# Five batches in place of eleven for the levels of a gated recurrence, with folded keys and queries copied into tiles of their own

## The reference, cut to what matters

```
f   = lb + (1 - lb) * sigmoid(z);   kin = 1 - f;   q = silu(q)
attn[i, j] = sum_k q[i, k] * kin[j, k] * prod_{j < t <= i} f[t, k]      (j <= i)
o[i]       = sum_j attn[i, j] * v[j]
o          = rms_norm(o) * gnorm * silu(g)
```

## Time and profile before

| what | value |
|---|---|
| median of 3 runs (lowest, highest) | 717.39 us (716.24, 717.43) |
| the profiled execution's own time | 716.37 us |
| its span, first to last instruction | 714.4 us |
| TensorE busy | 704.4 us, 99% of the span |
| VectorE, ScalarE, GpSimd busy | 439.6, 330.5, 139.3 us |
| granted TensorE clock, mean | 0.998 of full |

### The profile page before, as it was taken

How to read it: one execution, slowest core, us unless ns; L and a number is a source line. 1 busy time by engine, 2 the same in 40 slices (tenths; PEclk the granted TensorE clock), 3 DMA queues, 4 the chain that set the end, 5 groups by cost and what they waited for, 6 DMA issues and landing times.

```text
span 714.4 us, 10098 instructions
## 1 busy us (share of the span) xinstructions
PE 704.4 (99%) x3709; PEld 581.6 (81%) x3709; DVE 439.6 (62%) x706; ACT 330.5 (46%) x547; POOL 139.3 (20%) x106
## 2 busy tenths in 40 slices
PE   9999999999999999999999999999999999999995
PEld 6878878878888888888888888888888888888885
DVE  4774577697777655676766766767763333234546
ACT  5792534676676734534334333433332222226834
POOL 1015421076665512011011011011010000000000
PEclk9999999999999999999999999999999999999999
DMA  9433232332322114343333233333316232323202
GB/s 276 129 93 108 60 89 62 116 96 85 88 90 60 60 60 118 88 118 89 89 106 99 88 92 113 89 88 103 95 59 191 83 102 90 104 90 117 89 0 118
DMA packets 113454, 69.44 MB, mean 97 GB/s; under 512 B 2946, under 2 KB 108370, under 8 KB 113418
## 3 DMA queue, kind: packets, MB, share of 16 engines
q1 hardware_dynamic: 111406, 65.42, 30.8%
q10 hardware_dynamic: 2012, 3.52, 1.5%
HBM read 66.81 MB, written 2.13 MB: 96 GB/s over the span
## 4 chain that ended last, share of the span: by engine, by line
PE 95%; DVE 3%; issue 1%; ACT 1%; POOL 0%; DVEq 0%; ACTq 0%
PE bank L640 24%; PE bank L641 24%; PE bank L642 24%; PE bank L646 4%; PE bank L648 4%; PE bank L647 4%; PE bank L838 2%; PE bank L822 2%; PE bank L810 1%; PE bank L697 1%; PE bank L812 1%; PE bank L880 1%; PE bank L1062 0%; DVE b_kq L541 0%; PE bank L755 0%
## 5 line engine op out<-in xcount | busy, mean ns | idle before, releaser
L1122 ACT ACTIVATE w_hi<-raw 128x1024 fp32r<-128x1024 f32 (+1 forms) x104 | 107.9, 1039 | 221.0 <-PE bank L642 202.4
L640 PE MATMUL bank<-h_hi,w_hi 128*128 128x512 f32 x518 | 203.6, 393 | 0.0
L642 PE MATMUL bank<-h_hi,w_lo 128*128 128x512 f32 x518 | 202.0, 390 | 0.0
L641 PE MATMUL bank<-h_lo,w_hi 128*128 128x512 f32 x518 | 201.8, 390 | 0.0
L1572 DVE TENSOR_TENSOR w_lo<-raw,w_hi 128x1024 fp32r<-128x1024 f32 (+1 forms) x104 | 128.9, 1240 | 103.3 <-ACT w_hi L1122 103.2
L642 PEld LDWEIGHTS bank<-h_hi,w_lo 128*128 128x128 f32 x518 | 97.2, 188 | 20.6
L640 PEld LDWEIGHTS bank<-h_hi,w_hi 128*128 128x128 f32 x518 | 97.3, 188 | 20.2 <-issue 0.9
L641 PEld LDWEIGHTS bank<-h_lo,w_hi 128*128 128x128 f32 x518 | 97.3, 188 | 18.7
L2147 POOL TENSOR_SCALAR probs<-probs,row_inv 128x512 f32<-128x512 f32 (+3 forms) x48 | 67.1, 1403 | 65.4 <-DVE row_inv L1824 65.4
L2157 POOL TENSOR_TENSOR conv_v<-conv_g,conv_v 128x512 f32<-128x512 f32 x22 | 28.3, 1288 | 212.9 <-DVE conv_v L1701 212.9
L640 PE MATMUL bank<-act_hi,w_hi 128*128 128x512 f32 x176 | 68.6, 389 | 0.0
(11 more groups left out here) (279 smaller groups left out, 1032.5 us busy)
## 6 DMA issues: line engine op xcount, KB each, us to landing
raw<-in_w_up SPq DMA_DIRECT2D x44, 512.0 KB, 3.7
raw<-in_w_in SPq DMA_DIRECT2D x18, 512.0 KB, 3.8
raw<-in_w_down SPq DMA_DIRECT2D x16, 512.0 KB, 3.5
raw<-in_w_out SPq DMA_DIRECT2D x8, 512.0 KB, 3.4
raw<-in_w_pg SPq DMA_DIRECT2D x8, 512.0 KB, 3.7
raw<-in_w_in SPq DMA_DIRECT2D x8, 384.0 KB, 3.5
bias<-bias_table ACTq DMA_DIRECT2D x6, 512.0 KB, 3.6
raw<-in_w_down SPq DMA_DIRECT2D x8, 384.0 KB, 3.0
```

Of the source, the lines that this page charges most:

```text
L640: pe.matmul(bank, hi, x_hi, start=first, stop=False)
L641: pe.matmul(bank, hi, x_lo, start=False, stop=False)
L642: return pe.matmul(bank, lo, x_hi, start=False, stop=last)
L1122: act.activation(w_hi[:, u % SPLIT, 0:nk * ncol], raw[:, u % RAW, 0:nk * ncol], ACT.Copy)\
```

## The change

Rounds 2 to 5 (levels 1 to 4) go out together in slot 12 behind step 5, rounds 6 to 9 in slot 15 behind step 0, 10 and 11 behind step 7 of slot 15, 12 and 13 together in slot 16 behind step 4. Rounds 0 and 1 stay. Four PSUM banks serve them (`ROUND_BANK`). For this the folded operands get tiles of their own for four levels (`b_pack`, and for each fourth level `b_ktok` and `b_gate`): ScalarE now copies the queries too, four copies for a level in place of two (`fold`), one level in each of the slots 8 to 13. The decays of the next level now wait for these copies (`b_folded`) and no longer for the round; VectorE has one decay in each slot from 8 to 14, behind `split_lo`, two in slot 15. From level 5 on a fold also waits until the round that used its tile four levels ago is out. `flip_values` moves behind rounds 10 and 11, its copy to slot 16. The three Newton instructions of the second pair go one by one behind the first three ticks of slot 20, the fourth instruction behind its last tick.

```diff
-ROUND_AT = {8: ((3, (0, 1)),), 9: ((2, (2,)),), 10: ((2, (3,)),), 11: ((1, (4,)),), 12: ((1, (5,)),),
-            13: ((0, (6,)),), 14: ((0, (7,)),), 15: ((0, (8, 9)), (6, (10, 11))), 16: ((3, (12,)), (6, (13,)))}
+ROUND_AT = {8: ((3, (0, 1)),), 12: ((5, (2, 3, 4, 5)),), 15: ((0, (6, 7, 8, 9)), (7, (10, 11))), 16: ((4, (12, 13)),)}
+ROUND_BANK = (2, 3, 2, 3, 0, 1, 2, 3, 0, 1, 2, 3, 2, 3)
+DECAY_AT = {8: (1,), 9: (2,), 10: (3,), 11: (4,), 12: (5,), 13: (6,), 14: (7,), 15: (8, 9)}
+FOLD_AT = {8: 1, 9: 2, 10: 3, 11: 4, 12: 5, 13: 6}
+FOLDS = 4
...
         def decayed(eng, level, pair, done):
-            eng.wait_ge(b_scored, round_of(level - 1, pair) + 1)
+            if folded(level - 1):
+                eng.wait_ge(b_folded, 4 * (level - 1))
+            else:
+                eng.wait_ge(b_scored, round_of(level - 1, pair) + 1)
...
-            def fold_keys(level):
+            def fold(level):
                 s = 1 << (level - 1)
+                keys, queries = fold_tiles(level)
+                if level > FOLDS:
+                    act.wait_ge(b_scored, round_of(level - FOLDS, 0) + 1)
                 for pair, decays in enumerate((qk_ready, qk_other)):
-                    if level > 1:
-                        act.wait_ge(decays, level)
-                    act.activation(half_keys(b_keys, pair * s, s), half_keys(b_kin[:, pair, :], pair * s, s), ACT.Copy)\
+                    act.wait_ge(decays, level)
+                    act.activation(half_keys(keys, pair * s, s), half_keys(b_kin[:, pair, :], pair * s, s), ACT.Copy)\
+                       .then_inc(b_folded, 1)
+                    act.activation(half_keys(queries, (1 - pair) * s, s), half_keys(q_of(pair), (1 - pair) * s, s), ACT.Copy)\
                        .then_inc(b_folded, 1)
...
                 if slot == V_FIRST + V_STEPS // 2 - 1:
                     keep_value_bank(0, 0)
                     keep_value_bank(0, 1)
-                for n in rounds_in(slot):
-                    if folded(ROUND_OF[n][0]) and folded(ROUND_OF[n][0] + 1):
-                        fold_keys(ROUND_OF[n][0] + 1)
+                if slot in FOLD_AT:
+                    fold(FOLD_AT[slot])
...
+                    if slot == B_OUT_SLOT + 3:
+                        if i < 3:
+                            b_root(1, i)
+                        else:
+                            b_norm(1)
```

More of the change, by code:

```diff
@@ L136 @@
 V_BANKS = 2 * TT
-FLIP_SLOT = V_FIRST + V_STEPS // 2 + 1
 EARLY = ((0, 1, 2, 5, 3, 6), (0, 1, 2, 5, 3, 6, 4))
@@ L167, in kept_after, with bank_before @@
     return fill + 1 + min(max(fill - HALF_ROUND + 1, 0), 2)
+def bank_before(n):
+    return max((m for m in range(n) if ROUND_BANK[m] == ROUND_BANK[n]), default=None)
 def folded(level):
@@ L310, in build @@
         sb("after_small", [P, 40 - 4 * TT])
+        early = ExitStack()
+        b_pack = sb("b_pack", [P, 2 * (FOLDS - 1), 1024], F32, early)
+        early.close()
         mixing = ExitStack()
@@ L546, in half_keys, with fold_tiles @@
             return bass.AP(tensor=t.tensor, offset=t.offset + start, ap=[[t.ap[0][0], P], [2 * s, 512 // s], [1, s]])
-        b_keys = b_ktok[:, :, :, :].rearrange("p a b c -> p (a b c)")
-        def folded_queries(at, s):
-            return kq_at(2048 + at, [[2 * s, HEAD // (2 * s)], [1024 + s, 2], [1, s]])
+        def fold_tiles(level):
+            n = (level - 1) % FOLDS
+            if n == FOLDS - 1:
+                return b_ktok[:, :, :, :].rearrange("p a b c -> p (a b c)"), b_gate[:, :, :].rearrange("p a n -> p (a n)")
+            return b_pack[:, 2 * n, :], b_pack[:, 2 * n + 1, :]
         ATT_AT = {(b, b): b for b in range(TT)}
@@ L686, in b_round @@
                     if folded(level):
-                        pe.wait_ge(b_folded, 2 * level)
+                        pe.wait_ge(b_folded, 4 * level)
                 keys, queries = b_kin[:, pair, :], q_of(pair)
-                if n >= 2:
-                    pe.wait_ge(b_kept, kept_after(n - 2))
-                bank = score[n % 2]
+                if bank_before(n) is not None:
+                    pe.wait_ge(b_kept, kept_after(bank_before(n)))
+                bank = banks[ROUND_BANK[n]]
                 if folded(level):
-                    s = 1 << (level - 1)
+                    keys, queries = fold_tiles(level)
                     for c in range(2 * TT):
@@ L697, in b_round @@
                             mm = pe.matmul(bank[half * HEAD:(half + 1) * HEAD, c * HEAD:(c + 1) * HEAD],
-                                           b_keys[:, at:at + HEAD], folded_queries(at, s), start=True, stop=True)
+                                           keys[:, at:at + HEAD], queries[:, at:at + HEAD], start=True, stop=True)
                 elif level == 0:
@@ L725, in flip_values @@
             def flip_values():
-                wait_taken(pe, TT)
+                pe.wait_ge(b_kept, kept_after(9))
                 pe.wait_ge(v_kept, V_BANKS)
-                pe.matmul(banks[0][:, :], flip, b_v[:, 1, :, :].rearrange("p t c -> p (t c)"), start=True, stop=True).then_inc(v_flipped, 1)
+                pe.matmul(banks[ROUND_BANK[9]][:, :], flip, b_v[:, 1, :, :].rearrange("p t c -> p (t c)"), start=True, stop=True).then_inc(v_flipped, 1)
             def b_states():
@@ L856, in mixers @@
                             wait_taken(pe, WIDE - 1)
-                        if slot == FLIP_SLOT:
-                            flip_values()
                         for n in batch:
                             b_round(n)
+                        if batch[0] == 10:
+                            flip_values()
                 if slot == B_OUT_SLOT:
@@ L964, in _ @@
                 if u == V_LAST:
+                    pe.wait_ge(b_kept, kept_after(8))
+                if u == V_LAST + 1:
                     pe.wait_ge(flip_kept, 1)
@@ L1230, in keep_flipped @@
                 act.wait_ge(v_flipped, 1)
-                act.activation(b_v[:, 1, :, :], banks[0][:, :].rearrange("p (t c) -> p t c", t=TT), ACT.Copy).then_inc(flip_kept, 1)
+                act.activation(b_v[:, 1, :, :], banks[ROUND_BANK[9]][:, :].rearrange("p (t c) -> p t c", t=TT), ACT.Copy).then_inc(flip_kept, 1)
             def split_piece(slot, n):
@@ L1321, in mixers @@
                     split_piece(slot, 1)
-                if slot == ROUND_SLOT:
-                    act.wait_ge(kin_ready, B_HEADS)
-                    fold_keys(1)
                 if slot == V_FIRST + V_STEPS // 2 - 1:
@@ L1430, in beside_unit @@
                     keep_value_bank(0, 3)
-                if u == FLIP_SLOT + 1:
-                    keep_flipped()
                 if u == V_LAST:
@@ L1435, in beside_unit @@
                         keep_value_bank(1, t)
+                    keep_flipped()
                 if split_at(u) is not None and u + 2 < PG:
@@ L1773, in b_rest, with b_root @@
                    .then_inc(b_sq_lo, 1)
-            def b_norm(pair):
[L1777 to L1784, removed]
+            def b_root(pair, step):
+                v, r, c = b_tot[:, pair, 0:SEQ], b_tot[:, pair, SEQ:2 * SEQ], chunks_of(pair)
+                if step == 0:
+                    dve.wait_ge(b_rstd, pair + 1)
+                    dve.tensor_tensor(c, v, r, ALU.mult).then_inc(b_newton, 1)
+                elif step == 1:
+                    dve.wait_ge(b_newton, 3 * pair + 1)
+                    dve.tensor_tensor(c, c, r, ALU.mult).then_inc(b_newton, 1)
+                else:
+                    dve.wait_ge(b_newton, 3 * pair + 2)
+                    dve.scalar_tensor_tensor(out=v, in0=c, scalar=-3.0, in1=r, op0=ALU.add, op1=ALU.mult).then_inc(b_newton, 1)
+            def b_norm(pair):
+                v = b_tot[:, pair, 0:SEQ]
                 dve.wait_ge(b_newton, 3 * pair + 3)
@@ L1833, in mixers @@
             def mixers(slot):
+                decays = DECAY_AT.get(slot, ())
+                if decays:
+                    decayed(dve, decays[0], 0, qk_ready)
                 for at, batch in batches_in(slot):
-                    if at >= 4 and at == batches_in(slot)[0][0]:
-                        split_piece(slot, 0)
-                        split_piece(slot, 1)
                     for n in batch:
-                        level, pair = ROUND_OF[n]
-                        if level < LEVELS and pair == 0:
-                            decayed(dve, level + 1, 0, qk_ready)
+                        if n == 10:
+                            decayed(dve, LEVELS, 0, qk_ready)
                         keep_scores(n)
-                    if at < 4 and at == batches_in(slot)[0][0]:
-                        split_piece(slot, 0)
-                        split_piece(slot, 1)
                 if slot == B_OUT_SLOT - 2:
@@ L1873, in mixers @@
                         split_piece(slot, hh)
-                if slot in (B_OUT_SLOT + 1, B_OUT_SLOT + 2):
-                    b_norm(slot - B_OUT_SLOT - 1)
+                if slot == B_OUT_SLOT + 1:
+                    for step in range(3):
```

(2 more changed lines are left out.)

## The result

| what | before | after |
|---|---|---|
| median of 12 runs each (lowest, highest) | 716.98 us (716.24, 717.45) | 718.76 us (718.09, 719.08) |
| span of the profiled execution | 714.4 us | 716.3 us |
| its mean granted TensorE clock | 0.998 | 0.995 |

The ratio is 1.0023, with a 95% interval of 1.0015 to 1.0031: the change made the kernel 1.8 us slower. The forecast was 0.2 us faster.

What follows compares the result with a forecast made beforehand. TensorE bounds the kernel, busy 704.4 of 714.4 us. Gains of 3.7 us less a 3.5 us wait give 0.2 us faster: 717.39 to 717.2 us, own range 716.0 to 718.4, 8 in 10 from 714.7 to 718.9.

Steps and rivals of the forecast that it cites:

- second rival: Clock falls while TensorE waits in unit 12: 1.8 us more, 719.0 us, slower by 0.2%; chance 0.1.
- signs of being wrong: No gap in unit 12, `split_lo` at 1.2 us throughout, granted clock under 1.00 behind the gap, new gap in slots 15, 20, 21.
- The wait: TensorE in unit 12 waits from 82.9 to 86.4 for ScalarE to empty value bank 6: 3.5 us in two pieces.
- The chain as worked out: Preparing a level: GpSimd decay 2.3, blocked `split_lo` 1.07, VectorE decay 1.2, fold 2.3; 6.9 us against a 5.45 us slot.
- first rival: VectorE does not block behind GpSimd, a level takes 5.7, fold 4 ends at 82.0: gains stand alone, 713.7 us; chance 0.2.
- side remark: Slot 12: fold 4 ends at 85.6, rounds 2 to 5 want it at 84.3; alone a wait of 1.3 us.
- The gains: TensorE savings: 1.95 fewer batches, 0.2 slot 16, 0.40 level 1, 0.2 round 10, 0.94 second norm's root; 3.7 us.
- fixed price of a batch: TensorE pays 0.39 us to leave and enter the matmul stream; five fewer in slots 9 to 15 save 1.95 us.
- the 0.40: Level 1's round costs 1.71 us against level 4's 1.31; saved once its queries lie dense, bounds 0 and 0.40.
- The root: Second norm's Newton instructions spread behind ticks: turns of ticks 6 and 7 2.05 us apart, not 3.00; gain 0.94 us.
- forecast's own range: 716.0 to 718.4 us, from GpSimd decays at 2.3 to 2.5 and gains of root and slot 16 at their ends.
- wider one: The 8 in 10 range, reaching to the halves of the rivals: 714.7 to 718.9 us.

## Why the prediction was wrong

**The step that failed is the refusal of the second rival,** by which the sum put the clock at nothing: "the end of the span here shows that a gap has to be longer than 4 us before the clock falls, so I go by the row". A row at the end of the span shows one gap. It was read as the shortest gap that lowers the clock, and it is not: in unit 12 one of 2.6 us did it in each of 12 executions of the changed kernel (mean clock 0.994 or 0.995 in all), one of 2.7 us in nine of ten, one of 2.2 us in seven of ten, one of 1.5 us in none of eleven (mean clock 0.996 to 0.998 and 716.4 to 717.5 us, as the kernel before). Even the end of a span does not give one length. In the changed kernel:

```profile
708.00:709.00 1.00, 0.70 (x6) 0.50 (x5) 0.97 (x4) 0.86 (x2) 0.00 (x0) 1.00 0.01 0
...
711.00:712.00 1.00, 0.00 (x0) 0.00 (x0) 0.48 (x4) 0.53 (x3) 0.00 (x0) 0.98 0.65 266
```

TensorE's last matmul ends at 708.7, and a mean of 0.98 puts the fall just ahead of 712: some 3.3 us later, where the same working gives 4.4 for the earlier trace rows. The rival was priced well (1.8 us; 1.5 measured) and would have given 719.0; it got a chance of 0.1. A granted clock under 1.00 behind the gap stood among the prediction's own signs of being wrong.

The Trainium skill (TensorE: Matmul & The Clock Gate, "HAM oscillation — how this bites in real kernels") has idle gaps between bursts of matmuls put TensorE back to its half clock. This trace agrees (granted clock 0.50 behind a gap of 2.62 us), with a shorter wait than those that the section describes; for the length the measurement decides. The row that was set against the rule did not contradict it.

**The wait:** foreseen in its place, its releaser and its two pieces, 3.5 us; 3.80 measured. The chain as worked out, 6.9 us a level with `split_lo` blocked behind GpSimd, stands: splits of 3.03, 2.62 and 2.31 us, folds that end 6.6 to 7.5 us apart. Turning the order round showed that the split ahead of the decay makes the chain late. That run takes the whole split out of the chain, with its wait for ScalarE's `split_hi`; the share of the block alone was not run by itself. By the durations it is 3.03 + 2.62 + 2.31 - 3 x 1.23 = 4.27 us, without which fold 4 would have ended near 82.0 in place of 86.28, an estimate that agrees with the first rival's 82.0.

**A side remark was wrong:** fold 4's lateness "alone would be a wait of 1.3 us". It costs nothing, because three rounds of the batch go ahead of the one that needs it. With the copies of banks 6 and 7 ahead of fold 4 the second wait, 2.62 us, is gone: it came from where they stand in ScalarE's queue. The first, 0.86, stays there and goes only with the shorter chain.

**The gains:** 3.7 us foreseen; 2.74 + 1.06 = 3.80 by the traces of the changed kernel, and 4.0 (ratio 0.9944) where they stand alone. The fixed price of a batch, 0.39, was 0.36; four rounds in one batch, 0.39 + 4 x 0.92 = 4.07, took 4.11, with nothing extra for level 1 now that its queries lie dense. Before, `folded_queries` did more at level 1 than leave out every second element: it took one element at a time from two places 1025 apart in turn; which of the two cost the 0.40 was not tried. The root gave 1.06 for 0.94.

**The size of the error:** 3.80 + 1.70 - 3.80 = 1.7 us slower, of which 1.5 is the clock. Without it the forecast of no change would have held, as the runs with extra matmuls show (1.0005 and 1.0002). The 718.76 measured lies above the forecast's own range (716.0 to 718.4) and just inside the wider one (to 718.9), which says nothing for the mechanism. The forecast also started from 717.39, the median of three runs, 0.4 above that of twelve.

## What to carry to other kernels

Where two engines block each other, put the instruction that others wait for ahead of the one that has time: here that order alone is worth about 6 us, the clock's fall included. Before work is taken out of the bound engine's stream, ask what paced the others: the rounds that went had given the chain its time. A wait on TensorE is priced as its length plus what the clock may cost behind it; if it can't be avoided, fill it: five matmuls that nobody needs, 1.1 us of work, were enough here.

## What the runs showed of the hardware

The clock falls late: in one execution TensorE had worked again for more than 1 us when it went down, so the idle time itself reads 1.00, and the slow stretch, more than 3 us at half speed, lies wholly behind the gap. Which gap brings it about is not fixed: at 2.7 us of idle it fell in nine executions of ten, at 2.2 us in seven of ten. Why in these and not in the others was not tried.

VectorE and GpSimd block each other on these elementwise instructions, whichever starts first. A split that takes 1.23 us free took 2.31 to 3.03 beside a decay on GpSimd and ended about 1.1 us behind it; GpSimd's decay of level 3 took 2.44 us where it had started first (72.74 in the changed kernel) and 3.49 where VectorE's decay had started 0.05 us ahead of it (70.50, with VectorE's decay ahead of its split).
